# Where the on-chip tensors of a one-core transformer kernel lie: the weights' two parts moved behind the tables

## The reference

```
x = x + 0.5 * swiglu(rmsnorm(x), ffn_w_in, ffn_w_out)      # 1024 -> 2 x 2816 -> 1024
x = x + mixer(rmsnorm(x), ...)                             # HGRN2 in layer 0, MLA in layer 1
x = x + 0.5 * swiglu(rmsnorm(x), ffn_w_in, ffn_w_out)
x = x + sigmoid(rmsnorm(x) @ ple_w_gate) * (p @ ple_w_in)
...                                                        # shared latent keys and values between the layers
x = x + even_mixer(...); x = x + conv_ffn(...)             # stick-breaking attention and pooling
x = x + odd_mixer(...);  x = x + conv_ffn(...)             # gated linear attention
```

## The kernel before, in words

| tensor | start mod 2048 | start mod 128 |
|---|---|---|
| `w_hi`, `w_lo` (all slots) | 128 | 0 |
| `x_hi`, `x_lo` | 128 | 0 |
| `h_hi`, `h_lo` | 704 | 64 |
| `c_hi`, `c_lo`, `q_both`, `x_lo_2` | 1504 | 96 |

## Time and profile before

### The profile page before, as it was taken

How to read it: one execution, slowest core, us unless ns; L and a number is a source line. 1 busy time by engine, 2 the same in 40 slices (tenths; PEclk the granted TensorE clock), 3 DMA queues, 4 the chain that set the end, 5 groups by cost and what they waited for, 6 DMA issues and landing times.

```text
span 1857.5 us, 36683 instructions
## 1 busy us (share of the span) xinstructions
PE 1790.9 (96%) x14492; PEld 1759.8 (95%) x14492; DVE 1189.8 (64%) x1764; ACT 957.1 (52%) x1097; POOL 351.7 (19%) x280
## 2 busy tenths in 40 slices
PE   7999989989999999999999999989899999989999
PEld 7999989979999989998998999988899999989998
DVE  6555679986554665546545655565487776567776
ACT  5444667774434753445335444474365545655453
POOL 2000400030004600016564000467400011020001
PEclk9999989999999999999999999999899999999999
DMA  6556323335555355544343555433345453345452
GB/s 215 216 184 238 116 93 118 111 114 203 181 181 174 133 188 182 182 156 141 118 147 118 200 181 188 176 136 137 114 159 190 171 192 124 127 159 181 181 203 91
DMA packets 45168, 298.25 MB, mean 161 GB/s; under 512 B 5024, under 2 KB 5408, under 8 KB 15920
## 3 DMA queue, kind: packets, MB, share of 16 engines
q1 hardware_dynamic: 45104, 297.38, 45.2%
HBM read 296.31 MB, written 1.05 MB: 160 GB/s over the span
## 4 chain that ended last, share of the span: by engine, by line
PE 81%; DVE 10%; ACT 5%; issue 3%; DMA 1%; POOL 0%; SPq 0%; ACTq 0%; DVEq 0%
PE wk L380 15%; PE wk L381 15%; PE wk L382 15%; PE acc L380 8%; PE acc L381 8%; PE acc L382 8%; DVE sumsq L678 1%; PE wk L1032 1%; DVE x_lo L457 1%; PE wk L391 1%; PE wk L390 1%; PE wk L392 1%; ACT w_hi L326 1%; DVE x L422 1%; ACT tmp L619 1%
## 5 line engine op out<-in xcount | busy, mean ns | idle before, releaser
L326 ACT ACTIVATE w_hi<-raw 128x2048 fp32r<-128x2048 f32 (+5 forms) x300 | 532.5, 1783 | 432.2 <-PE wk L382 358.3
L381 PE MATMUL wk<-x_lo,w_hi 128*128 128x256 f32 x2560 | 727.1, 284 | 0.0
L380 PE MATMUL wk<-x_hi,w_hi 128*128 128x256 f32 x2208 | 632.0, 286 | 17.8 <-DVE x_lo L457 11.3
L2602 POOL TENSOR_TENSOR w_lo<-raw,w_hi 128x512 fp32r<-128x512 f32 (+1 forms) x274 | 351.0, 1316 | 1490.9 <-ACT w_hi L326 1490.8
L382 PE MATMUL wk<-x_hi,w_lo 128*128 128x256 f32 x2208 | 627.0, 284 | 0.0
L352 DVE TENSOR_TENSOR w_lo<-raw,w_hi 128x2048 fp32r<-128x2048 f32 (+2 forms) x218 | 484.1, 2222 | 170.2 <-ACT w_hi L326 170.2
L381 PEld LDWEIGHTS wk<-x_lo,w_hi 128*128 128x128 f32 x2560 | 492.1, 192 | 0.4
L380 PEld LDWEIGHTS wk<-x_hi,w_hi 128*128 128x128 f32 x2208 | 425.1, 193 | 21.2 <-DVE x_lo L457 12.5
L382 PEld LDWEIGHTS wk<-x_hi,w_lo 128*128 128x128 f32 x2208 | 424.9, 192 | 0.0
L380 PE MATMUL acc<-h_hi,w_hi 128*128 128x256 f32 x1376 | 392.2, 285 | 16.3 <-DVE h_lo L2191 4.8
L381 PE MATMUL acc<-h_lo,w_hi 128*128 128x256 f32 x1376 | 387.7, 282 | 0.0
(11 more groups left out here) (323 smaller groups left out, 2146.5 us busy)
## 6 DMA issues: line engine op xcount, KB each, us to landing
raw<-w_ffn_loop SPq DMA_DIRECT2D x120, 1024.0 KB, 4.8
raw<-w_conv_loop SPq DMA_DIRECT2D x60, 1024.0 KB, 4.8
raw<-w_mla_loop SPq DMA_DIRECT2D x18, 768.0 KB, 4.3
raw<-w_hgrn_loop SPq DMA_DIRECT2D x10, 896.0 KB, 4.5
raw<-w_ple_gate SPq DMA_DIRECT2D x8, 1024.0 KB, 4.8
raw<-w_odd_loop SPq DMA_DIRECT2D x10, 768.0 KB, 4.2
raw<-w_even_loop SPq DMA_DIRECT2D x6, 1024.0 KB, 4.8
raw<-w_odd_proj SPq DMA_DIRECT2D x6, 1024.0 KB, 4.8
```

The source lines that it names most:

```text
L326: nc.scalar.activation(w_hi[slot][:, 0:n], raw[slot][:, 0:n], ACT.Copy).then_inc(S("hi_ready"), 1)
L380: nc.tensor.matmul(dst, hi, a_hi, start=start, stop=False, skip_group_check=True)
L381: nc.tensor.matmul(dst, hi, a_lo, start=False, stop=False, skip_group_check=True)
L2602: last = nc.gpsimd.tensor_tensor(w_lo[slot][:, a:b], raw[slot][:, a:b], w_hi[slot][:, a:b].bitcast(F32), ALU.subtract)
```

## The change

No instruction is added, removed or moved, on any engine: the built programs list the same instructions in the same order. What changes is the order in which the on-chip tensors are allocated. The two parts of the weights go from their place behind `raw` to a place behind `x`, h, the latents, the parameters, the constants and a few rows of statistics; h and the latents come forward, right behind `x_lo`.

```
         raw = [sb(f"raw{s}", [P, SLOT_TILES * P]) for s in range(SLOTS)]
-        w_hi = [sb(f"w_hi{s}", [P, SLOT_TILES * P], F32R) for s in range(SLOTS)]
-        w_lo = [sb(f"w_lo{s}", [P, SLOT_TILES * P], F32R) for s in range(SLOTS)]
         x = sb("x", [P, KD, SEQ])
         x_hi = sb("x_hi", [P, KD, SEQ], F32R)
         x_lo = sb("x_lo", [P, KD, SEQ], F32R)
+        h_hi = sb("h_hi", [P, 2, SEQ], F32R)
+        h_lo = sb("h_lo", [P, 2, SEQ], F32R)
+        h_val = sb("h_val", [P, 2, SEQ])
+        c_hi = sb("c_hi", [P, 2, SEQ], F32R)
+        c_lo = sb("c_lo", [P, 2, SEQ], F32R)
+        q_both = sb("q_both", [P, KD, SEQ], F32R)
+        x_lo_2 = sb("x_lo_2", [P, KD, SEQ], F32R)
         par = sb("par", [P, N_PARAMS])
         cst = sb("cst", [P, N_CONSTS])
         rstd = sb("rstd", [P, SEQ])
...
         ln_tok = sb("ln_tok", [P, 2 * TB])
-        h_hi = sb("h_hi", [P, 2, SEQ], F32R)
-        h_lo = sb("h_lo", [P, 2, SEQ], F32R)
-        h_val = sb("h_val", [P, 2, SEQ])
-
+        w_hi = [sb(f"w_hi{s}", [P, SLOT_TILES * P], F32R) for s in range(SLOTS)]
+        w_lo = [sb(f"w_lo{s}", [P, SLOT_TILES * P], F32R) for s in range(SLOTS)]
         tmp = sb("tmp", [P, 8, SEQ])
...
-        c_hi = sb("c_hi", [P, 2, SEQ], F32R)
-        c_lo = sb("c_lo", [P, 2, SEQ], F32R)
-        q_both = sb("q_both", [P, KD, SEQ], F32R)
...
-        x_lo_2 = sb("x_lo_2", [P, KD, SEQ], F32R)
```

## The result

| | before | after |
|---|---|---|
| median of four runs each | 1855.6 us | 1831.7 us |
| lowest to highest | 1853.9 to 1857.4 | 1826.7 to 1840.4 |
| ratio, 95% interval | | 0.9875 [0.9848, 0.9902] |
| span of the profiled execution | 1857.5 us | 1824.9 us |

The change made the kernel 23.9 us faster. The forecast was 16 us, 1840, with a range down to 1833: the direction and the mechanism (a shorter distance between the matmuls of the streams) came as forecast, and the size did not. The profiled execution happens to be the fastest of the four, so its 32.6 us against the profile of before are more than the medians show.

What follows compares the result with a forecast made beforehand. PE's matmul start distance was taken to bound the six feed-forward loops. Savings of 12.1 us there and 3.8 us outside, sum 15.9, took the 1856.1 us median to 1840; own range 1834 to 1847, 8-in-10 range 1833 to 1858.

Steps and rivals of the forecast that it cites:

- What bounds the kernel, and what can change: In the six feed-forward loops, time is matmul count times start distance; the change alters that distance or moved tensors' access durations.
- item 4: ACT, DVE and POOL accesses to moved tensors: taken as 0, with 1.9 us either way outside the loops.
- d = 0 and 32 give 120.0, 64 less: Matmul pace in ns by stationary start minus moving start, mod 128 bytes: 120.0 at 0 and 32, 117.9 at 64.
- Item 1: 8928 matmuls with x, q or c moving, or x stationary, go to d = 64, each 120.0 to 117.9 ns.
- Item 2: 4128 matmuls with h moving stay at d = 64 with the operands' sides exchanged: 0 ns.
- If the sign counts: Caveat for h moving at the reversed distance: 2.1 ns more per matmul, or down to 110.6 ns.
- The share on the path: All 5760 loop matmuls count, 12.1 us; the other 3168, in mixers, gates, heads and tails, count partly, 3.8 us.
- share of 57%: Outside the six loops, PE's part of the chain, 473 of 825 us, used to scale the gain there.
- no change: Rival: the 2.1 ns belong to what is computed, not its place; every stream keeps its distance, 1856 us; chance 0.13.
- slower: Rival: only the moving operand's place counts; x and q stay at 120 ns, h loses 2.1 ns, 1864 us; chance 0.14.
- More: Rival: the moving read's whole addition vanishes, streams run at 110.6 ns, 1759 us; chance 0.04.
- rung at 116 ns: Streams going only some way towards 110.6 ns, to 116 ns, priced at 1822 us.

Runs made afterwards that it cites:

- the two halves of the change: Against the kernel before: only the weights' parts moved, 1828.3 us; only h, the latents, q_both and x_lo_2 moved forward, 1863.3 us.
- the kernel at -64: Against the kernel before: weights' parts stay behind raw, x, h, c, q_both and x_lo_2 displaced to 64 mod 128 bytes; 1839.8 us, ratio 0.9919.
- the runs at 96 and 80: Changed kernel with weights' parts sliced from an offset, 96 or 80 bytes behind a multiple of 128; 1844.3 us and 1850.9 us.
- the one at 48: Changed kernel with weights' parts sliced from an offset, 48 bytes behind a multiple of 128; 1860.7 us, ratio 1.0028.

## Why the prediction was wrong

- **What bounds the kernel, and what can change**: right. PE's busy time fell and nothing else did. DVE's and ACT's busy time in the loops stayed within a microsecond, which was item 4's 0.
- **d = 0 and 32 give 120.0, 64 less; the displacement of the stationary operand works too**: right for 0 and 64, shown by the two halves of the change and by the kernel at -64; for 32 no further run was made.
- **Item 1, the price of 2.1 ns**: the step that failed. It took 117.9 ns, read from h at d = -64, for what the change makes, d = +64, since both are 64 mod 128. The runs show that in one and the same placing a stream has two paces, 117.8 and 113.4 ns, and they agree with a distance that counts with its sign, mod 256. At -64 nearly all channel streams of the kernel take the first; at +64 many take the second. Where the second was taken a matmul gained 6.6 ns and not 2.1. The 117.9 was one stretch of h of the 87, and three others of them ran at 113.4 in the same trace.
- **Item 2, 0 for h** "with the sides exchanged": failed for the same reason. "If the sign counts" stood there, with a bound of 110.6, and was not carried into the forecast's own range. In a fast loop h falls from 117.9 to 113.4 as well.
- **The share on the path**: right for the loops. Their 5760 matmuls give 12.1 us at the forecast's price; the two fast loops add (1296 + 1440) x 4.4 ns = 12.0, in sum 24.1 against the 1037.3 - 1012.9 = 24.4 measured. Outside the loops the forecast had 3.8 us, and the two profiles of the changed kernel gained 8.2 and 6.6. Some streams there are at the second pace, so the share of 57% is not tested by it.
- **The rivals**: no change and slower are out for the whole change; the slower case is what half of it does. "More" had 4% and a rung at 116 ns, 1822; by its own counts that rung comes to 1819 (7566 x 4.0 and 3591 x 1.9 ns, 37 us). The changed kernel, a mixture of the two paces, lies between it and the forecast. The range ended at 1833 because the larger gain was left out of it; a placing whose distance no row showed should have kept part of the way down to 110.6.
- **The Trainium skill's rule of the two ports** ("TensorE: Matmul & The Clock Gate", "Part 2: What happens when you issue a matmul"): the runs disagree with it for this form. The loads of the stationary operand and the moving read do not go on independently of each other: by their distance the second loop takes 172.8 us at d = 0 and 169.6 or 163.4 at 64.

What stays open: why +64 and -64 differ in how often the fast pace is entered, which of the neighbours of a loop's first matmul decide it, whether it is the width or the number of the clears that matters, and why the profiles of the changed kernel agree in their fast loops. The changed kernel's times spread from 1826.7 to 1840.4; the mean granted clock was 0.992 in the fastest run and 0.985 in the slowest, but 0.992 also in one of 1831.5, so the clock alone does not order them, and how much falls to it and how much to the pace of loops was not separated.

## What to carry to other kernels

Where PE runs long streams with a new stationary operand for each matmul, read the distance between the starts, not the busy time, and look at it for each pair of operands by their addresses: here the remainder of their distance was worth 120.0, 117.8 or 113.4 ns a matmul, 5% of a loop. Take the addresses from the built program: a description by plain sizes was off by 80 bytes here, and the runs at 96 and 80 gained 11 and 5 us, and the one at 48 lost 6. A stream can have two stable paces: look at what stands right ahead of a long loop, and before trusting one number for a placing, look at several streams and several executions.

## What the runs showed of the hardware that was not expected

- Two stable paces of one stream, 113.4 and 117.8 ns for 256 moving columns at d = 64 mod 128; 120.0 at 0 and 32. With `w_lo` 128 bytes aside of `w_hi` mod 256: 120.0 at 48, 118.9 (some streams 117.8) at 80, 117.8 at 96.
- Eight matmuls of 256 columns at d = 0, in place of four of 512 also at d = 0, ahead of a stream at d = +64 brought the fast pace into all four loops where it had been missing, and at d = -64 into three.
- 2.1 us of idle time on PE ahead of the third loop were followed by 3.6 us at a granted clock of 0.53 in one kernel and by full clock in another; 3.3 us there were followed by 6 us at 0.53.
- A DVE instruction with two operands in SBUF took 7.02 us instead of 1.3 to 1.6 while POOL had a run of its own subtractions. "SBUF — State Buffer", "SBUF: two separate sides" of the Trainium skill describes a port pair that DVE and GpSimd hold one at a time for a whole instruction; the row agrees in kind, though it lasts through most of a run of six POOL instructions (7.53 us) and not one. In the kernel of 1839.8 us the same instruction took 1.79 us inside such a run, so the page's rule alone does not explain the 7.02. No run was made on it.
